# Attention stage of a two-layer decoder step: transposes and value products three units behind the scores, exponentials one unit behind

## The chip, the cores and the metric

The kernel runs as one program on one core of a Trainium2 chip. The metric is the device time of one execution in microseconds. A core has TensorE for matrix products (PE in the profile; PEld are its weight loads), VectorE (DVE), ScalarE (ACT), GpSimd (POOL), and SyncE (SP), which here only issues DMAs.

## The reference, cut to what matters

The program is one inference step of a decoder with two layers, for a prompt of 1024 rows and eight samples of one row. Layer 0 is RWKV-7 mixing and an MLP, then shared keys and values are projected, and layer 1 is differential attention over them and an MLP. The change touches the attention stage alone. For the prompt, that stage computes for each of 8 heads and each block of 128 query rows

```python
s = jnp.einsum('bqhmd,bkhmd->bhmqk', qi, k).astype(jnp.float32) * ATTN_SCALE   # m: two maps per head
s = jnp.where(k_pos[None, :] <= q_pos[:, None], s, NEG)
p = jax.nn.softmax(s, axis=-1)
attn = p[..., 0, :, :] - lam * p[..., 1, :, :]
o = jnp.einsum('bhqk,bkhe->bqhe', attn, v)
```

and each row of `o` is divided by its root mean square and scaled. For the samples it does the same with one query row each over 1024 past keys and values, which lie in pages of 128 rows that a table names, 64 pages in all.

## The kernel before, in words

`attention_phase` runs five instruction streams, one for each engine, that meet only in semaphores; each engine executes its own stream in order. The work is cut into 64 units (`NU`): unit u is head u // 8 and one block of 128 query rows, in the order of `ORDER`, so that a unit has 8, 1, 7, 2, 6, 3, 5, 4 blocks of keys in turn. Even units are "long" (5 to 8 blocks), odd ones "short" (1 to 4). The two kinds have buffers of their own: the scores of a long unit lie in four PSUM banks, those of a short one in two, and there is one buffer for the probabilities, one for the combined probabilities (`at`, in the profile att_attn_long and att_attn_short) and one for their transposed blocks (`aT`, att_attn_cols) of each kind. All transposes, of whatever, go through one PSUM bank, `tb`, and ScalarE must copy it out before TensorE may fill it again; all value products go through one bank, `ob`. In the profile both are named aux.

Every stream loops over u from 0 to `END` - 1. With w = u - 2 an iteration does:

- TensorE: transposes of the first four blocks of unit w (L2088, through `turn4`), the score products of unit u for both maps and the causal mask (L2106, L2110), transposes of the other blocks of w, then `extras(u)`, then the value products of w (L2120). The extras are transposes of the next head's keys and values (`rows`), of the finished head's output (`fin`), and for the samples page score transposes and, from unit 38 on, every third unit, value products of a sample (`page_v`, L2155) and a fold of their result (`page_cols`, L2162).
- VectorE: the maximum of the scores of unit u (L2231) and its negative scaled (L2233), a page sum (L2250), `combine(u - 1)`, which is a reciprocal (L2239), a ratio of one element per row (L2241) and the combined probabilities (L2245), and a second page sum.
- ScalarE: copies of the transposed blocks of w (L2355), copies for the extras, the scaled output of w (`take`, L2362), the exponentials of unit u for both maps (L2347).
- GpSimd: for u below 32, two products of a page of past keys with a query row (L2072), each into one of two buffers that VectorE's page sums read; and once a head the squares of its output (L2078).
- SyncE: loads of the next head, of key pages four ahead, and of value pages.

What orders the two sides is a few waits in this code: TensorE's transposes of w wait for `combine(w)`, its score products of u for the exponentials of u - 2, ScalarE's exponentials for L2233 of the same unit.

```python
            for u in range(END):
                w = u - 2
                live = 0 <= w < NU
                if live:
                    need(pe, "attn", w + 1)
                    turn4(("attn", w, 0), [...])
                if u < NU:
                    scores(u)
```

## Time and profile before

| | us |
|---|---|
| median of 3 runs (lowest, highest) | 4176.69 (4170.09, 4177.06) |
| the profiled execution: its time | 4166.23 |
| its span, first to last instruction | 4164.5 |
| attention stage in it, first DMA issue to the next stage's first | 2593.1 to 3205.8 |
| TensorE busy over the span (share) | 3483.6 (84%) |
| VectorE, ScalarE, GpSimd busy | 1899.8, 1346.4, 1563.1 |

Times in the trace count from the start of the span. The attention stage is 612.7 us of it. A row of a timeline gives the start, the time taken, the engine, the line of the code, the operation with output and input, and in brackets how long the engine had been idle and what released it. Consecutive instructions of VectorE overlap by a little under 0.1 us in such rows, so that what an instruction costs its engine is the distance to the start of the next. A row of a view of waits gives the waiting instruction and the one it waited for, then the total, the number of waits and the longest. The score product of unit u is recognised by the maximum that follows it (L2231).

### The profile page before, as it was taken

How to read it: one execution, taken by the hardware profiler on the slowest of the kernel's cores; microseconds unless marked ns; L12 is line 12 of the kernel's file. 1: busy time of each engine (PE TensorE's matmuls, PEld its weight loads, DVE VectorE, ACT ScalarE, POOL GpSimd, SP SyncE). 2: the span in 40 equal slices, each digit the busy share in tenths (PEclk: the TensorE clock that was granted, in tenths of full speed). 3: DMA queues.
4: the chain of work that ended last, by engine and by line, in shares of the span. 5: the costliest groups of instructions: out<-in, count | busy, mean ns of one | idle time of the engine just before them, and what ended most of it. 6: DMA issues, size and time to landing. Idle time of an engine off the chain costs nothing. (4 is left out here: it accounts for less than half of the span.)

```text
span 4164.5 us, 78261 instructions
## 1 busy us (share of the span) xinstructions
PE 3483.6 (84%) x34038; PEld 3147.2 (76%) x34038; DVE 1899.8 (46%) x2159; ACT 1346.4 (32%) x2059; POOL 1563.1 (38%) x648
## 2 busy tenths in 40 slices
PE   5889686898897298999999999455775989999896
PEld 2888435888786188999999998333443889999896
DVE  3333606455542586353454430677433772522622
ACT  1111113433432134333333433333444333333332
POOL 0111000000000155656656665455000656556563
PEclk8999858999998599999999999667887999999998
DMA  5222123334331543445444665545353534444442
GB/s 191 83 85 73 46 92 126 122 113 149 114 105 48 167 124 115 133 131 152 141 138 140 183 188 158 193 152 202 137 202 102 163 104 139 127 138 140 125 141 71
DMA packets 710476, 546.83 MB, mean 131 GB/s; under 512 B 34763, under 2 KB 667491, under 8 KB 709885
## 3 DMA queue, kind: packets, MB, share of 16 engines
q1 hardware_dynamic: 664182, 473.18, 36.9%
q10 hardware_dynamic: 45606, 67.55, 4.7%
q8 instruction: 266, 4.36, 0.4%
q0 software_dynamic: 352, 1.18, 0.1%
q14 instruction: 70, 0.57, 0.0%
HBM read 471.55 MB, written 70.29 MB: 130 GB/s over the span
## 5 line engine op out<-in xcount | busy, mean ns | idle before, releaser
L1630 POOL TENSOR_TENSOR dense_w_lo<-dense_w_raw,dense_w_hi 128x1024 fp32r<-128x1024 f32 x504 | 1273.4, 2532 | 974.8 <-ACT dense_w_hi L1701 974.6
L1686 PE MATMUL acc<-dense_x_hi,dense_w_hi 128*128 128x344 f32 x2496 | 813.2, 330 | 86.2 <-DVE dense_x_lo L1791 41.4
L1687 PE MATMUL acc<-dense_x_lo,dense_w_hi 128*128 128x344 f32 x2496 | 802.3, 326 | 0.0
L1701 ACT ACTIVATE dense_w_hi<-dense_w_raw 128x1024 fp32r<-128x1024 f32 x504 | 531.1, 1056 | 628.8 <-PE acc L1691 536.0
L1686 PEld LDWEIGHTS acc<-dense_x_hi,dense_w_hi 128*128 128x128 f32 x2496 | 482.4, 193 | 98.6 <-issue 79.7
L1687 PEld LDWEIGHTS acc<-dense_x_lo,dense_w_hi 128*128 128x128 f32 x2496 | 482.6, 193 | 2.5 <-issue 0.9
L1686 PE MATMUL acc<-dense_hid_hi,dense_w_hi 128*128 128x344 f32 x1536 | 483.4, 319 | 0.5 <-DVE dense_hid_lo L1811 0.5
L1687 PE MATMUL acc<-dense_hid_lo,dense_w_hi 128*128 128x344 f32 x1536 | 483.4, 319 | 0.0
L1691 PE MATMUL acc<-dense_x_hi,dense_w_lo 128*128 128x344 f32 x2496 | 449.7, 323 | 1.3 <-POOL dense_w_lo L1630 1.3
L1691 PEld LDWEIGHTS acc<-dense_x_hi,dense_w_lo 128*128 128x128 f32 x2496 | 409.9, 190 | 2.1 <-POOL dense_w_lo L1630 1.8
L750 POOL TENSOR_TENSOR x0T<-nT,levels 128x512 f32<-128x512 f32 x16 | 29.7, 1855 | 744.0 <-DVE bR L1249 744.0
L1686 PEld LDWEIGHTS acc<-dense_hid_hi,dense_w_hi 128*128 128x128 f32 x1536 | 288.4, 188 | 1.1 <-DVE dense_hid_lo L1811 1.1
L1687 PEld LDWEIGHTS acc<-dense_hid_lo,dense_w_hi 128*128 128x128 f32 x1536 | 288.2, 188 | 0.0
L170 PE MATMUL acc<-mix_hi,w_hi 128*128 128x344 f32 (+2 forms) x672 | 221.7, 330 | 76.8 <-DVE mix_lo L538 61.4
L1807 DVE TENSOR_TENSOR dense_relu<-dense_relu 128x344 f32<-128x344 f32 x192 | 148.6, 774 | 292.8 <-ACT dense_relu L1717 292.5
L1826 DVE SCALAR_TENSOR_TENSOR z<-acc,mods,z 128x344 f32<-128x344 f32 (+1 forms) x144 | 81.1, 568 | 431.5 <-PE acc L1691 431.5
L1691 PE MATMUL acc<-dense_hid_hi,dense_w_lo 128*128 128x344 f32 x1536 | 274.2, 321 | 1.0 <-POOL dense_w_lo L1630 1.0
L1691 PEld LDWEIGHTS acc<-dense_hid_hi,dense_w_lo 128*128 128x128 f32 x1536 | 249.5, 188 | 1.6 <-POOL dense_w_lo L1630 1.6
L1717 ACT ACTIVATE dense_relu<-acc 128x344 f32<-128x344 f32 x192 | 87.4, 455 | 460.4 <-PE acc L1691 362.4
L2072 POOL TENSOR_TENSOR att_k_prod<-att_k_page,att_q_row_all 128x1024 f32<-128x1024 f32 x64 | 153.4, 2400 | 176.0 <-DVE att_scores L2250 144.8
L171 PE MATMUL acc<-mix_lo,w_hi 128*128 128x344 f32 (+2 forms) x672 | 217.9, 324 | 0.0
L172 PE MATMUL acc<-mix_hi,w_lo 128*128 128x344 f32 (+2 forms) x672 | 217.7, 324 | 0.0
(384 smaller groups left out, 5983.6 us busy)
## 6 DMA issues: line engine op xcount, KB each, us to landing
dense_w_raw<-in_ffn_w SPq DMA_DIRECT2D x384, 512.0 KB, 4.1
ada_quarter<-in_ada_w SPq DMA_DIRECT2D x40, 1024.0 KB, 11.0
att_k_page<-in_cache_k SPq DMA_DIRECT2D x64, 512.0 KB, 3.6
att_v_page<-in_cache_v SPq DMA_DIRECT2D x64, 512.0 KB, 5.9
scratch_mix<-proj_stage ACTq DMA_DIRECT2D x48, 516.0 KB, 2.7
scratch_mix<-dense_stage ACTq DMA_DIRECT2D x72, 172.0 KB, 2.1
w_raw<-in_a_w_rkv SPq DMA_DIRECT2D x24, 512.0 KB, 4.2
dense_w_raw<-in_a_w_o SPq DMA_DIRECT2D x24, 512.0 KB, 4.5
```

What stands on the lines that cost most here:

```text
L170: m.nc.tensor.matmul(out, hi, xh[:, k, cols], start=(k == 0), stop=False)
L171: m.nc.tensor.matmul(out, hi, xl[:, k, cols], start=False, stop=False)
L172: last = m.nc.tensor.matmul(out, lo, xh[:, k, cols], start=False, stop=(k == KC - 1))
L1630: nc.gpsimd.tensor_tensor(wlo[:, i % NW], raw[:, i % NRAW], whi[:, i % NW].bitcast(F32), ALU.subtract).then_inc(S("lo"), 1)
L1686: T_.matmul(out, whi[:, s % NW, k, :], a, start=j.first and k == 0, stop=False)
L1687: T_.matmul(out, whi[:, s % NW, k, :], b, start=False, stop=False)
L1691: last = T_.matmul(out, wlo[:, s % NW, k, :], a, start=False, stop=j.last and k == KC - 1)
L1701: A(whi[:, i % NW], raw[:, i % NRAW], ACT.Copy).then_inc(S("hi"), 1)
L1717: A(t[:, n % 2, :], bank(jobs[s].acc), ACT.Relu).then_inc(S("taken"), 1)
L1807: V.tensor_tensor(tt, tt, tt, ALU.mult).then_inc(S("hid_sq"), 1)
L1826: V.scalar_tensor_tensor(zk, ps[:, 0:w], m.mod(gt, j.mo), zk, ALU.mult, ALU.add).then_inc(S("added"), 1)
L2072: nc.gpsimd.tensor_tensor(prod[:, j % 2, :], kp[:, j % NK, :], qb[:, b % 2, :], ALU.mult).then_inc(S("prod"), 1)
```

## The change

The lag of transposes and value products behind the scores becomes `LAG` = 3 in every stream, and what has to live longer gets more buffers: two combined-probability buffers of each kind, four slots for maxima, sums and ratios. With an odd lag, the transposes of a short unit meet the scores of a long one. ScalarE issues the exponentials of unit u - 1 in iteration u, map 0 behind the first copy of transposed blocks and map 1 behind the second. TensorE splits the value products of a long unit in two, and puts the first extra of an iteration between the parts, or, with a short unit, ahead of its value products. GpSimd's page products get a third buffer (`NR`). The ratio becomes a `tensor_scalar` with two column operands. At the start of the stage the mask, keys and queries are loaded first, and the scores of unit 0 go ahead of the sample transposes, which now share four banks. The once-a-head steps of the output's root mean square move one unit later.

```diff
-        NK, NV = 4, 12
+        NK, NV, NR = 4, 12, 3
...
-        END = NU + 10
+        END, LAG = NU + 10, 3
...
-        at = (sb("attn_long", [P, SEQ]), sb("attn_short", [P, SEQ // 2]))
+        at = (sb("attn_long", [P, 2, SEQ]), sb("attn_short", [P, 2, SEQ // 2]))
...
-        mx, nb, l, rl, w1 = (sb(x, [P, 2, 2]) for x in ("max", "neg_max", "sums", "weights", "ratio"))
+        mx, nb, l, rl, w1 = (sb(x, [P, 4, 2]) for x in ("max", "neg_max", "sums", "weights", "ratio"))
...
-        kp, prod = sb("k_page", [P, NK, D]), sb("k_prod", [P, 2, D])
+        kp, prod = sb("k_page", [P, NK, D]), sb("k_prod", [P, NR, D])
...
+        def attn_of(u):
+            return at[kind(u)][:, (u // 2) % 2]
+
+        def pages_of(u):
+
+            return range(min(NPAGE, 2 * u), min(NPAGE, 2 * u + 2))
...
-            nc.sync.dma_start(tab[:], io["page_table"].rearrange("(o b) n -> o (b n)", o=1)).then_inc(S("table_in"), 16)
+            nc.sync.dma_start(causal[:], io["masks"][:, C_CAUSAL:C_CAUSAL + P]).then_inc(S("mask_in"), 16)
+            nc.sync.dma_start(k[:, 0], m.scr[S_K, 0, :, 0:SEQ]).then_inc(S("in_k"), 16)
+            nc.sync.dma_start(q[:, 0], m.scr[S_R, 0, :, 0:SEQ]).then_inc(S("in_q"), 16)
             for t, row in ((qs, S_R), (ks, S_K), (vs, S_V)):
                 nc.sync.dma_start(t[:], m.scr[row, :, :, SEQ:T].rearrange("c p n -> p c n")).then_inc(S("cols_in"), 16)
-            nc.sync.dma_start(k[:, 0], m.scr[S_K, 0, :, 0:SEQ]).then_inc(S("in_k"), 16)
-            nc.sync.dma_start(q[:, 0], m.scr[S_R, 0, :, 0:SEQ]).then_inc(S("in_q"), 16)
+            nc.sync.dma_start(tab[:], io["page_table"].rearrange("(o b) n -> o (b n)", o=1)).then_inc(S("table_in"), 16)
             nc.sync.dma_start(v[:], m.scr[S_V, 0, :, 0:SEQ]).then_inc(S("in_v"), 16)
-            nc.sync.dma_start(causal[:], io["masks"][:, C_CAUSAL:C_CAUSAL + P]).then_inc(S("mask_in"), 16)
             for i, name in enumerate(("b_lam_q", "b_lam_k")):
...
-                if u < KU:
-                    for j in (2 * u, 2 * u + 1):
-                        b = j // NP
-                        pool.wait_ge(S(f"k_in{j % NK}"), 16 * (j // NK + 1))
-                        if j % NP == 0:
-                            pool.wait_ge(S(f"qb{b % 2}"), 16 * (b // 2 + 1))
-                        need(pool, "red", j - 1)
-                        nc.gpsimd.tensor_tensor(prod[:, j % 2, :], kp[:, j % NK, :], qb[:, b % 2, :], ALU.mult).then_inc(S("prod"), 1)
-                if u % KC == 2 and u > 2:
+                for j in pages_of(u):
+                    b = j // NP
+                    pool.wait_ge(S(f"k_in{j % NK}"), 16 * (j // NK + 1))
+                    if j % NP == 0:
+                        pool.wait_ge(S(f"qb{b % 2}"), 16 * (b // 2 + 1))
+                    need(pool, "red", j - NR + 1)
+                    nc.gpsimd.tensor_tensor(prod[:, j % NR, :], kp[:, j % NK, :], qb[:, b % 2, :], ALU.mult).then_inc(S("prod"), 1)
+                if u % KC == 3 and u > 3:
                     h = u // KC - 1
                     if h < NH:
...
-            def values(w):
+            def values(w, part):
                 h, n = w // KC, blocks(w)
-                need(pe, "take", w)
-                need(pe, "t_in", nth["rows", h, 3] + 1)
-                for j in range(n):
-                    if j % 4 == 0:
-                        need(pe, "t_in", nth["attn", w, j // 4] + 1)
+                if part == 0:
+                    need(pe, "take", w)
+                    need(pe, "t_in", nth["rows", h, 3] + 1)
+                need(pe, "t_in", nth["attn", w, part] + 1)
+                for j in range(4 * part, min(n, 4 * part + 4)):
                     last = T_.matmul(ob[:, 0:P], aT[kind(w)][:, j * P:(j + 1) * P], vrow[:, h % 2, j, :],
                                      start=(j == 0), stop=(j == n - 1))
-                last.then_inc(S("o_mm"), 1)
+                if j == n - 1:
+                    last.then_inc(S("o_mm"), 1)
...
+            need(pe, "consts", 2)
+            need(pe, "in_k", 16)
+            scores(0)
             pe.wait_ge(S("cols_in"), 48)
-            for i, t in enumerate((qs, ks, vs)):
-                for h in range(NH):
-                    last = T_.transpose((m.acc[0], m.acc[1], m.aux2)[i][0:NS, h // 4, (h % 4) * P:(h % 4 + 1) * P], t[:, h, :], m.ident[:])
-            last.then_inc(S("qkv_t"), 1)
-            need(pe, "sample_rows", 3)
+            sample_turn(qs, six[:, 4:6, :])
+            sample_turn(ks, m.aux2)
+            need(pe, "sample_rows", 1)
+            sample_turn(vs, six[:, 4:6, :])
+            need(pe, "sample_rows", 2)
             need(pe, "consts", 4)
             for part in range(4):
                 head_rows(0, part)
+            need(pe, "sample_rows", 3)
             for u in range(END):
-                w = u - 2
+                w = u - LAG
                 live = 0 <= w < NU
                 if live:
                     need(pe, "attn", w + 1)
-                    turn4(("attn", w, 0), [at[kind(w)][:, j * P:j * P + P] for j in range(min(4, blocks(w)))])
-                if u < NU:
+                    turn4(("attn", w, 0), [attn_of(w)[:, j * P:j * P + P] for j in range(min(4, blocks(w)))])
+                if 0 < u < NU:
                     scores(u)
+                todo = extras(u)
                 if live and blocks(w) > 4:
-                    turn4(("attn", w, 1), [at[kind(w)][:, j * P:j * P + P] for j in range(4, blocks(w))])
-                for name in extras(u):
+                    turn4(("attn", w, 1), [attn_of(w)[:, j * P:j * P + P] for j in range(4, blocks(w))])
+                    values(w, 0)
+                elif live and todo:
+                    extra(todo.pop(0))
+                    values(w, 0)
+                elif live:
+                    values(w, 0)
+                if live and blocks(w) > 4:
+                    if todo:
+                        extra(todo.pop(0))
+                    values(w, 1)
+                for name in todo:
                     extra(name)
-                if live:
-                    values(w)
```

On VectorE (buffer indices aside) and on ScalarE:

```diff
             def combine(u):
-                kd, n = kind(u), blocks(u) * P
+                kd, c, n = kind(u), u % 4, blocks(u) * P
                 need(dve, "exp", 2 * u + 2)
-                need(dve, "take", u - 1)
-                V.reciprocal(rl[:, kd, :], l[:, kd, :]).then_inc(S("rl"), 1)
+                need(dve, "take", u - 3)
+                V.reciprocal(rl[:, c, :], l[:, c, :]).then_inc(S("rl"), 1)
                 need(dve, "rl", u + 1)
-                V.scalar_tensor_tensor(w1[:, kd, 0:1], rl[:, kd, 1:2], lam[:, 0:1], l[:, kd, 0:1], ALU.mult, ALU.mult).then_inc(S("ratio"), 1)
+                V.tensor_scalar(w1[:, c, 0:1], rl[:, c, 1:2], l[:, c, 0:1], lam[:, 0:1], ALU.mult, ALU.mult).then_inc(S("ratio"), 1)
                 need(dve, "ratio", u + 1)
-                if u >= 2:
-                    need(dve, "t_mm", nth[attn_rounds(u - 2)[-1]] + 1)
-                V.scalar_tensor_tensor(at[kd][:, 0:n], pm[kd][:, 1, 0:n], w1[:, kd, 0:1], pm[kd][:, 0, 0:n], ALU.mult,
+                if u >= 4:
+                    need(dve, "t_mm", nth[attn_rounds(u - 4)[-1]] + 1)
+                V.scalar_tensor_tensor(attn_of(u)[:, 0:n], pm[kd][:, 1, 0:n], w1[:, c, 0:1], pm[kd][:, 0, 0:n], ALU.mult,
                                        ALU.add).then_inc(S("attn"), 1)
...
-                if u < KU:
-                    page_sums(2 * u + 1)
-                if r == 3 and 1 <= h <= NH:
+                for j in todo:
+                    page_sums(j)
+                if r == 4 and 1 <= h <= NH:
                     need(dve, "osq", h)
                     need(dve, "rrms", h - 1)
                     V.tensor_reduce(ss[:], osq[:], AX.X, ALU.add).then_inc(S("ss"), 1)
-                if r == 4 and 1 <= h <= NH:
+                if r == 5 and 1 <= h <= NH:
                     need(dve, "rms", h)
                     need(dve, "on", h - 1)
                     V.reciprocal(rs[:], ss[:]).then_inc(S("rrms"), 1)
...
-            need(act, "qkv_t", 1)
-            for i in range(3):
-                A(rows[:, i, :].rearrange("p (a n) -> p a n", a=2), (m.acc[0], m.acc[1], m.aux2)[i][0:NS, 0:2, :],
-                  ACT.Copy).then_inc(S("sample_rows"), 1)
+            for i, banks in enumerate((six[:, 4:6, :], m.aux2, six[:, 4:6, :])):
+                need(act, "qkv_t", i + 1)
+                A(rows[:, i, :].rearrange("p (a n) -> p a n", a=2), banks[0:NS], ACT.Copy).then_inc(S("sample_rows"), 1)
...
-            def exps(u):
-                kd, n = kind(u), blocks(u) * P
+            def exps(u, maps):
+                kd, c, n = kind(u), u % 4, blocks(u) * P
                 need(act, "nb", u + 1)
                 need(act, "attn", u - 1)
-                for mp in range(2):
-                    A(pm[kd][:, mp, 0:n], scores_of(u, mp), ACT.Exp, bias=nb[:, kd, mp:mp + 1], scale=ATTN_SCALE,
-                      accum_out=l[:, kd, mp:mp + 1]).then_inc(S("exp"), 1)
+                for mp in maps:
+                    A(pm[kd][:, mp, 0:n], scores_of(u, mp), ACT.Exp, bias=nb[:, c, mp:mp + 1], scale=ATTN_SCALE,
+                      accum_out=l[:, c, mp:mp + 1]).then_inc(S("exp"), 1)
...
             for u in range(END):
-                w = u - 2
-                for name in attn_rounds(w):
-                    turned(name)
+                w = u - LAG
+                for i in range(2):
+                    for name in attn_rounds(w)[i:i + 1]:
+                        turned(name)
+                    if 1 <= u <= NU:
+                        exps(u - 1, (i,))
                 for name in extras(u):
                     extra(name)
                 if 0 <= w < NU:
                     take(w)
-                if u < NU:
-                    exps(u)
                 h, r = divmod(u, KC)
-                if r == 3 and 1 <= h <= NH:
+                if r == 4 and 1 <= h <= NH:
                     need(act, "ss", h)
                     A(ss[:], ss[:], ACT.Sqrt, bias=eps[:, 0:1], scale=1.0 / P).then_inc(S("rms"), 1)
```

On TensorE before, two iterations near the end of the second head, a long unit's transposes beside a long unit's scores and a short one's beside a short one's. The rows are iteration 14 (w = 12, scores of 5 blocks) and 15 (w = 13, scores of 4); att_o is the `fin` extra:

```order
L2088 MATMUL aux<-ident,att_attn_long 128x128 x4
L2106 MATMUL acc<-att_k,att_q 128x512 x2
L2106 MATMUL acc<-att_k,att_q 128x128 x2
L2110 MATMUL acc<-att_causal_r,att_eye_r 128x128 x2
L2088 MATMUL aux<-ident,att_attn_long 128x128 x2
L2088 MATMUL aux<-ident,att_o 128x128 x4
L2120 MATMUL aux<-att_v_rows,att_attn_cols_long 128x128 x6
L2088 MATMUL aux<-ident,att_attn_short 128x128 x3
L2106 MATMUL acc<-att_k,att_q 128x512 x2
L2110 MATMUL acc<-att_causal_r,att_eye_r 128x128 x2
L2088 MATMUL aux<-ident,att_o 128x128 x4
L2120 MATMUL aux<-att_v_rows,att_attn_cols_short 128x128 x3
```

There the extra stands ahead of all value products, and a turn of the bank follows a turn of the bank. In the changed kernel iterations 13 (w = 10, scores of 3 blocks) and 14 (w = 11, scores of 5 blocks); att_v is a `rows` extra:

```order
L2093 MATMUL aux<-ident,att_attn_long 128x128 x4
L2111 MATMUL acc<-att_k,att_q 128x384 x2
L2115 MATMUL acc<-att_causal_r,att_eye_r 128x128 x2
L2093 MATMUL aux<-ident,att_attn_long 128x128 x3
L2125 MATMUL aux<-att_v_rows,att_attn_cols_long 128x128 x4
L2093 MATMUL aux<-ident,att_v 128x128 x4
L2125 MATMUL aux<-att_v_rows,att_attn_cols_long 128x128 x3
L2093 MATMUL aux<-ident,att_attn_short 128x128 x2
L2111 MATMUL acc<-att_k,att_q 128x512 x2
L2111 MATMUL acc<-att_k,att_q 128x128 x2
L2115 MATMUL acc<-att_causal_r,att_eye_r 128x128 x2
L2093 MATMUL aux<-ident,att_o 128x128 x4
```

The value products (L2125) now stand between two uses of the transpose bank, and the seven blocks of the long unit w = 10 are transposed beside the short scores. On ScalarE before, iterations 14 and 15; att_probs are the exponentials, att_out_cols the copies of the `fin` extra:

```order
L2355 ACTIVATE att_attn_cols_long<-aux 128x512
L2355 ACTIVATE att_attn_cols_long<-aux 128x256
L2373 ACTIVATE att_out_cols<-aux,att_subln_g 128x512
L2362 ACTIVATE att_o<-aux,att_weights 128x128
L2347 ACTIVATE att_probs_long,att_sums<-acc,att_neg_max 128x640 x2
L2355 ACTIVATE att_attn_cols_short<-aux 128x384
L2373 ACTIVATE att_out_cols<-aux,att_subln_g 128x512
L2376 DMA scratch_mix<-att_out_cols 128x1024
L2362 ACTIVATE att_o<-aux,att_weights 128x128
L2347 ACTIVATE att_probs_short,att_sums<-acc,att_neg_max 128x512 x2
```

Both maps stand behind `take` (L2362). In the changed kernel the same engine, iterations 15 and 16, from the first copy of transposed blocks of w = 12:

```order
L2379 ACTIVATE att_attn_cols_long<-aux 128x512
L2371 ACTIVATE att_probs_long,att_sums<-acc,att_neg_max 128x640
L2379 ACTIVATE att_attn_cols_long<-aux 128x256
L2371 ACTIVATE att_probs_long,att_sums<-acc,att_neg_max 128x640
L2397 ACTIVATE att_out_cols<-aux,att_subln_g 128x512
L2400 DMA scratch_mix<-att_out_cols 128x1024
L2386 ACTIVATE att_o<-aux,att_weights 128x128
L2379 ACTIVATE att_attn_cols_short<-aux 128x384
L2371 ACTIVATE att_probs_short,att_sums<-acc,att_neg_max 128x512 x2
L2386 ACTIVATE att_o<-aux,att_weights 128x128
```

The exponentials of the long unit 14 are now one map behind each copy, and `take` comes last.

## Rows read from the trace of the kernel before

**Rows 1.** Busy us by stretch: PE, PEld, DVE, ACT, POOL, TensorE clock, DMA share, GB/s

```profile
2618.40:2925.80 307.40, 168.99 (x754) 109.89 (x754) 234.12 (x231) 102.77 (x235) 154.42 (x66) 0.69 0.51 177
2925.80:3181.90 256.10, 200.60 (x1151) 127.19 (x1150) 96.23 (x178) 116.87 (x267) 7.57 (x4) 0.83 0.39 138
```

**Rows 2.** Waits, VectorE and TensorE, 2771.8 to 2850.3: total us, times, longest

```profile
DVE att_max L2231 <- PE acc L2110: 21.1, 8, 4.2
PE aux L2088 <- DVE att_attn_long L2245: 20.0, 4, 6.0
PE aux L2088 <- DVE att_attn_short L2245: 12.5, 4, 5.7
```

**Rows 3.** Timeline, VectorE and GpSimd, one unit: start, us taken, engine, line

```profile
2778.56 1.21 DVE L2250 TENSOR_REDUCE att_scores<-att_k_prod 128x16 f32<-128x1024 f32 x1
...
2779.91 2.35 POOL L2072 TENSOR_TENSOR att_k_prod<-att_k_page,att_q_row_all 128x1024 f32<-128x1024 f32 x1 [2.08 <-DVE att_scores L2250]
...
2781.20 0.42 DVE L2231 TENSOR_REDUCE att_max<-acc 128x2 f32<-128x256 f32 x1 [1.43 <-PE acc L2110]
...
2781.65 0.63 DVE L2233 TENSOR_SCALAR att_neg_max<-att_max 128x2 f32<-128x2 f32 x1
...
2782.20 1.20 DVE L2250 TENSOR_REDUCE att_scores<-att_k_prod 128x16 f32<-128x1024 f32 x1
...
2783.52 2.39 DVE L2241 SCALAR_TENSOR_TENSOR att_ratio<-att_weights,att_neg_lambda,att_sums 128x1 f32<-128x1 f32 x1
...
2783.55 2.34 POOL L2072 TENSOR_TENSOR att_k_prod<-att_k_page,att_q_row_all 128x1024 f32<-128x1024 f32 x1 [1.29 <-DVE att_scores L2250]
...
2785.94 1.28 DVE L2245 SCALAR_TENSOR_TENSOR att_attn_long<-att_probs_long,att_ratio 128x1024 f32<-128x1024 f32 x1
...
2787.14 1.21 DVE L2250 TENSOR_REDUCE att_scores<-att_k_prod 128x16 f32<-128x1024 f32 x1
```

**Rows 4.** Lines of VectorE, 2925.8 to 3181.9: count, busy us, mean ns, idle before

```profile
L2231 DVE TENSOR_REDUCE att_max<-acc 128x2 f32<-128x2048 f32 (+7 forms) x32 | 43.4, 1357 | 152.8 <-PE acc L2110 152.8
...
L2245 DVE SCALAR_TENSOR_TENSOR att_attn_long<-att_probs_long,att_ratio 128x1024 f32<-128x1024 f32 (+3 forms) x15 | 16.5, 1098 | 0.5
...
L2245 DVE SCALAR_TENSOR_TENSOR att_attn_short<-att_probs_short,att_ratio 128x512 f32<-128x512 f32 (+3 forms) x16 | 8.8, 552 | 0.6
...
L2233 DVE TENSOR_SCALAR att_neg_max<-att_max 128x2 f32<-128x2 f32 x31 | 5.2, 169 | 1.1
...
L2272 DVE TENSOR_TENSOR att_o<-att_o,att_rms 128x1024 f32<-128x1024 f32 x4 | 4.9, 1225 | 0.1
```

**Rows 5.** Timeline of the stage's start (columns as in Rows 3)

```profile
2604.78 1.90 ACT L2320 ACTIVATE att_v_page<-acc 8x1024 f32<-8x1024 f32 x2
...
2613.87 4.65 POOL L2072 TENSOR_TENSOR att_k_prod<-att_k_page,att_q_row_all 128x1024 f32<-128x1024 f32 x2 [31.15 <-DMA att_q_row_all<-scratch_sample_y]
...
2635.11 2.02 DVE L2231 TENSOR_REDUCE att_max<-acc 128x2 f32<-128x1792 f32 x1 [3.76 <-PE acc L2110]
```

**Rows 6.** Waits of TensorE, 2925.8 to 3181.9 (columns as in Rows 2)

```profile
PE aux L2088 <- ACT att_attn_cols_short L2355: 13.7, 8, 2.6
PE aux L2088 <- ACT att_attn_cols_long L2355: 7.8, 12, 0.8
PE aux L2120 <- ACT att_attn_cols_short L2355: 6.3, 3, 2.5
PE aux L2155 <- ACT att_page_o L2388: 5.7, 8, 0.7
PE aux L2088 <- DVE att_attn_short L2245: 3.2, 2, 2.5
```

**Rows 7.** Lines of ScalarE, 2925.8 to 3181.9 (columns as in Rows 4)

```profile
L2347 ACT ACTIVATE att_probs_long<-acc,att_neg_max 128x1024 f32<-128x1024 f32 (+3 forms) x32 | 30.2, 950 | 1.0 <-DVE att_neg_max L2233 0.9
```

**Rows 8.** Timeline, one group of score products at either clock

```profile
2749.33 2.51 PE L2106 MATMUL acc<-att_k,att_q 64*128 64x512 f32 x8
...
2965.75 1.35 PE L2106 MATMUL acc<-att_k,att_q 64*128 64x512 f32 x8
```

30 lines of the change are left out of this document (17 added, 13 removed).

## The prediction, put on record before the changed kernel ran

> **What bounds the kernel now.** The busy times by stretch come first. The attention stage has two parts. In the first, from the maximum of unit 0 to that of unit 32 (307.4 us, 9.6 a unit), no engine is full: TensorE 169.0 us at a granted clock of 0.69, VectorE 234.1, GpSimd 154.4. In the second, to the maximum of unit 63 (256.1 us, 8.3 a unit), TensorE is busy for 200.6 us and nobody else for half the time [rows 1]. So the question is who waits for whom, and in the third head, a period of 78.5 us for eight units, the views of waits answer it: VectorE waits 21.1 us for score products (8 waits, of which one of 4.2 belongs to the period before, so 17), TensorE 32.5 us for combined probabilities [rows 2]. They take turns. TensorE's score products of unit u stand behind the transposes of u - 2, these behind `combine(u - 2)`, this behind the maximum of u - 1. A ring over both engines is what bounds the first part.
>
> VectorE has a second partner. In the timeline, each page sum (L2250) that ends lets GpSimd start its next page product 0.14 us later, and the product takes 2.34. While it runs, the reciprocal and the reductions keep their times, but the negative maximum took 0.63 us instead of 0.17, and the ratio, one element per row, took 2.39 and ended with the product [rows 3, 4] (the 0.17 is the mean of the second part, where GpSimd is idle). So two small things of a unit can each be held until a product ends.
>
> **First part, step by step.** With a lag of 3, TensorE's transposes in iteration u need `combine(u - 3)`, a whole iteration of VectorE earlier, and its score products need only the exponentials of u - 2. It gets ahead, and VectorE's wait for the scores goes: this alone would be 17 us a head. What is late next is VectorE itself with GpSimd. One unit, from the start of its preceding page sum, in distances between starts [rows 3]: the page product that this sum releases ran from 1.35 to 3.70 (2778.56 to 2779.91 and 2782.26); the maximum starts at 1.13 (the sum's 1.21 less the overlap) and takes 1.36 on average [rows 4], for a long unit of 8 blocks 2.3 by my estimate (eight forms from 0.42 for one block, in proportion); the negative maximum is held by the product, so the next page sum starts at 3.64 (2778.56 to 2782.20) whatever the size of the unit. Before, an idle wait stood in the place of much of this hold, 1.43 us in this unit. From there to the combined probabilities 3.74 (2782.20 to 2785.94, again the length of a product), then their own 0.74, the mean of 1.10 and 0.55 [rows 4] less the overlap of 0.08. Sum 8.12 us a unit. The ratio as a `tensor_scalar` changes nothing here: if it isn't held, the combined probabilities behind it are, by the same product; between 0 and 0.03 us a unit.
>
> Once a head come a multiplication of 1.23 us [rows 4] that waits for a product first, 2.8 us together beyond what a unit has anyway, and, estimated from the same holds, 1.5 us for GpSimd's squares in the middle of its products and for ScalarE's square root, which now waits in the middle of the stream for a sum that stands at the end of VectorE's iteration, with the exponentials of the next unit behind it. So a head takes 8 x 8.12 + 4.3 = 69.3 us. The third buffer of page products gains nothing: no row shows VectorE waiting for a product. From the maximum of unit 2 (2635.1 [rows 5]) to that of unit 32 (2925.8) there are 30 units and three such sets: 243.6 + 12.9 = 256.5 for 290.7, that is -34.
>
> Can TensorE keep up? Its busy time is 169.0 over 32 units, 5.3 a unit, all at the low clock; with a bare wait for the bank (0.7, below) twice a unit it needs 6.7 of 8.1. Yes, with 1.4 to spare.
>
> The start: the score products of unit 0 go ahead of the sample transposes, which ScalarE's copies (2604.8) wait for; eight score products take 2.51 us at the low clock [rows 8], and so I put the query row, and GpSimd's first product (2613.9 [rows 5]), 2.6 us later, at 2616.5. Two page products (4.65 [rows 5]) and a sum behind it the maximum of unit 1 is at 2622.3, and that of unit 2, after one normal unit, at 2630.4 for 2635.1, where it had waited 3.76 us for its scores: -5, with bounds of 0 and -8. First part: -39. Its bounds are 0 (the hold eats all that the idle gave) and -73 (17 us a head, and 5).
>
> **Second part.** Here VectorE waits for scores (152.8 us [rows 4]) and has no say. TensorE is idle for 256.1 - 200.6 = 55.5 us [rows 1]. Three kinds [rows 6]. Eleven waits, 13.7 + 6.3 = 20.0 us, 1.8 each, are for copies of a short unit's blocks: ScalarE has just begun the exponentials of a long unit, 0.95 us a map [rows 7], and they stand ahead of the copy. In the new order at most one map stands there, and score products or value products are between; I take them down to a bare round trip of 0.7: -12. The waits for combined probabilities, 3.2 us and smaller ones, go: -4. The rest, some 31 us, are bare round trips through the one bank, 0.65 (7.8 over 12) to 0.71 (5.7 over 8) each. Value products now stand between two of them in most iterations, but only one to four of them. Half goes: -15. Against that, ScalarE's wait for the sum of squares in the middle of its stream, 1.5 us four times: +6. Second part: -25, bounds +12 (each of 16 long units waits 0.75 more for a copy behind an exponential) and -55 (no idle time left). The tail after unit 63 has the same work with one iteration without scores more: 0, up to +2.
>
> **The sum.** -39 - 25 = -64 us on the profiled execution: 4166.2 to 4102. The median of the runs is 4176.7, 10.5 above the profiled one; the forecast in terms of the median is 4113.
>
> **Rivals.**
> 1. VectorE's idle time goes in full, because the products of GpSimd fall elsewhere than at the negative maximum. For it: with a third buffer GpSimd has a product more in hand and need not start one at the end of every sum. Against: it has 8.1 us for 4.7 us of work, so it is always caught up, and starts at a sum's end as in both cases of rows 3. -73 - 25 = -98: 4079. Chance 0.10.
> 2. The second part gives nothing: ScalarE's stream is in order, and a copy that had the exponentials of another unit ahead of it now has a map of its own iteration ahead. -39: 4138. Chance 0.16.
> 3. The clock rises as above: 4098. Chance 0.17.
> 4. Slower: the exponentials of u - 1 stand between the two copies of ScalarE, so TensorE's value products and its next bank wait for the negative maximum of u - 1, and the score products of u + 1 come behind them. If that ring (negative maximum, two maps 1.9, copy 0.6, extra, value products and transposes 4, scores 2.5, maximum 1.4, hold 2.3, and waits of 0.1 to 0.2 between closes once for every unit instead of once in two, it is about 13.7 us against 9.6 now in the first part. It decides from the point where more than one unit in five closes it (4.1 us lost against 1.0 gained). With half the units of the first part, 16 x 4.1 - 16 x 1.5 - 5 = +37, and no gain in the second: 4214. Against it: score products of u + 1 need the exponentials of u - 1 only, and by the order of the streams these are issued an iteration earlier. Chance 0.04.
> 5. The lag has no effect since page products and VectorE's own work fill the time that TensorE's part leaves: within 0.2% of now, 4177. Chance 0.03.
>
> **From these the numbers.** The forecast has 0.50, with a range of its own of 4095 to 4130. The range of 4078 to 4150 takes in the clock, the full recovery of the idle time and a second part without gain. All cases but the last two are faster by more than 0.2% (8 us, about what a measurement here can tell from no change): 0.93; 0.03 the same; 0.04 slower.
>
> **What would show it.** In the first part: no wait of VectorE for score products beyond a few, no wait of TensorE for combined probabilities longer than 1 us, the negative maximum at about 1 us on average for 0.45, a distance of 8.1 us between maxima. A distance of 7 would be rival 1, over 9 rival 4 or 5. In the second: TensorE's idle time at 30 us for 55, its waits for copies of short units near 0.7 each; the clock still near 0.83. The forecast is wrong if VectorE still waits for scores in the first part, or if ScalarE shows waits for the negative maximum in most units.

## The result, and the profile after

| | median us | lowest to highest | runs |
|---|---|---|---|
| before | 4173.4 | 4166.5 to 4177.1 | 4 |
| after | 4075.7 | 4070.8 to 4078.5 | 4 |

The ratio is 0.9767, 95% interval 0.9749 to 0.9784: 97.7 us faster, where 64 were forecast, and 2.3 us below the low end of the range. In the two profiled executions the attention stage, from its first DMA issue to the next stage's first, shrank from 612.7 to 515.4 us, by 97.3. The times of these two executions differ by 89.6 us, since in the changed kernel's the stage began 8.7 us later. Such shifts of the stage's start, up to 12.5 us, came between the traces of this study, whatever the kernel. So stretches of the stage are compared, not spans.

| stretch, from maximum to maximum | before | after | change | forecast |
|---|---|---|---|---|
| stage's start to unit 2 | 42.0 | 35.1 | -6.9 | -5 |
| first part, unit 2 to 32 | 290.7 | 235.5 | -55.2 | -34 |
| second part, unit 32 to 63 | 256.1 | 221.9 | -34.2 | -25 |
| tail | 23.9 | 22.9 | -1.0 | 0 |

First the changed kernel's busy times by stretch (columns as in [rows 1], whose first row begins 16.7 us earlier, at unit 0). First part, then second:

```profile
2636.94:2872.43 235.49, 144.04 (x720) 101.78 (x719) 226.39 (x221) 96.31 (x224) 149.20 (x63) 0.76 0.65 218
2872.43:3094.30 221.87, 181.61 (x1146) 117.18 (x1147) 99.33 (x179) 115.86 (x266) 7.58 (x4) 0.89 0.45 159
```

In the first part VectorE is now busy for 226.4 of 235.5 us, counting the time in which an instruction of it is held by GpSimd's product: it is the bound. In the second TensorE idles for 40.3 us (221.9 - 181.6), and its clock is 0.89.

The waits of the third head, 2746.3 to 2810.85, a period of 64.6 us where it was 78.5:

```profile
POOL att_k_prod L2077 <- DVE att_scores L2274: 24.1, 15, 2.4
...
PE aux L2093 <- DVE att_attn_long L2269: 11.9, 3, 4.9
ACT att_ss L2436 <- DVE att_ss L2291: 11.3, 1, 11.3
PE aux L2093 <- ACT att_attn_cols_long L2379: 9.8, 3, 7.3
```

VectorE's wait for score products, first in [rows 2] with 21.1, is gone: the view has no row of it. TensorE waits instead, for VectorE's combined rows and for the copies behind ScalarE's square root, and that costs nothing while VectorE is the bound. Where VectorE's time went over the whole first part is told by its lines. Before:

```profile
L2241 DVE SCALAR_TENSOR_TENSOR att_ratio<-att_weights,att_neg_lambda,att_sums 128x1 f32<-128x1 f32 x30 | 52.2, 1741 | 1.1
L2231 DVE TENSOR_REDUCE att_max<-acc 128x2 f32<-128x1792 f32 (+7 forms) x31 | 43.0, 1387 | 69.8 <-PE acc L2110 69.8
L2245 DVE SCALAR_TENSOR_TENSOR att_attn_long<-att_probs_long,att_ratio 128x896 f32<-128x896 f32 (+3 forms) x15 | 29.9, 1990 | 0.5
L2233 DVE TENSOR_SCALAR att_neg_max<-att_max 128x2 f32<-128x2 f32 x30 | 12.9, 430 | 1.0
L2245 DVE SCALAR_TENSOR_TENSOR att_attn_short<-att_probs_short,att_ratio 128x128 f32<-128x128 f32 (+3 forms) x15 | 8.1, 538 | 0.5
```

And after:

```profile
L2255 DVE TENSOR_REDUCE att_max<-acc 128x2 f32<-128x1792 f32 (+7 forms) x31 | 42.6, 1373 | 0.1
L2269 DVE SCALAR_TENSOR_TENSOR att_attn_long<-att_probs_long,att_ratio 128x896 f32<-128x896 f32 (+3 forms) x15 | 35.3, 2352 | 0.5
L2269 DVE SCALAR_TENSOR_TENSOR att_attn_short<-att_probs_short,att_ratio 128x128 f32<-128x128 f32 (+3 forms) x15 | 34.8, 2323 | 0.5
L2257 DVE TENSOR_SCALAR att_neg_max<-att_max 128x2 f32<-128x2 f32 x30 | 32.7, 1089 | 1.0
L2265 DVE TENSOR_SCALAR att_ratio<-att_weights,att_sums,att_neg_lambda 128x1 f32<-128x1 f32 x30 | 8.2, 273 | 1.1
L2263 DVE RECIPROCAL att_weights<-att_sums 128x2 f32<-128x2 f32 x30 | 4.5, 150 | 5.7 <-ACT att_probs_long L2371 5.7
```

Read by rows: the wait before the maximum -69.7; the negative maximum +19.8, since GpSimd's product now falls upon it more often; ratio and combined probabilities together from 90.2 to 78.3, -11.9; a new wait of the reciprocal for exponentials +5.7. Their sum, -56.1, is nearly the whole of -55.2. The new wait comes once a head, 1.9 us, where the exponentials stand behind the square root (the 11.3 of ScalarE in the waits above). The holds can be seen in one unit (columns as in [rows 3]):

```profile
2746.20 2.27 DVE L2255 TENSOR_REDUCE att_max<-acc 128x2 f32<-128x2048 f32 x1
...
2748.71 1.21 DVE L2274 TENSOR_REDUCE att_scores<-att_k_prod 128x16 f32<-128x1024 f32 x1
...
2750.03 0.27 DVE L2265 TENSOR_SCALAR att_ratio<-att_weights,att_sums,att_neg_lambda 128x1 f32<-128x1 f32 x1
2750.06 2.34 POOL L2077 TENSOR_TENSOR att_k_prod<-att_k_page,att_q_row_all 128x1024 f32<-128x1024 f32 x1 [1.29 <-DVE att_scores L2274]
...
2750.33 2.62 DVE L2269 SCALAR_TENSOR_TENSOR att_attn_short<-att_probs_short,att_ratio 128x512 f32<-128x512 f32 x1
...
2752.87 1.21 DVE L2274 TENSOR_REDUCE att_scores<-att_k_prod 128x16 f32<-128x1024 f32 x1
...
2754.00 0.41 DVE L2255 TENSOR_REDUCE att_max<-acc 128x2 f32<-128x256 f32 x1
...
2754.22 2.35 POOL L2077 TENSOR_TENSOR att_k_prod<-att_k_page,att_q_row_all 128x1024 f32<-128x1024 f32 x1 [1.82 <-DVE att_scores L2274]
2754.45 2.15 DVE L2257 TENSOR_SCALAR att_neg_max<-att_max 128x2 f32<-128x2 f32 x1
...
2756.51 1.21 DVE L2274 TENSOR_REDUCE att_scores<-att_k_prod 128x16 f32<-128x1024 f32 x1
```

From page sum to page sum over the maximum it is 3.64 (2752.87 to 2756.51), the forecast's number; over the combination 4.16 (2748.71 to 2752.87), where the forecast had 4.48. The ratio runs beside the product's start and isn't held (0.27). The 512-wide combination is, 2.62 for 0.75 alone, and ends 0.55 after the product.

TensorE's waits in the second part, against [rows 6]:

```profile
PE aux L2093 <- ACT att_attn_cols_long L2379: 8.0, 7, 1.9
PE aux L2093 <- ACT att_page_o L2412: 6.5, 8, 0.8
...
PE aux L2093 <- DMA att_k<-scratch_mix: 3.7, 1, 3.7
PE aux L2093 <- DVE att_scores L2274: 3.2, 1, 3.2
PE aux L2093 <- ACT att_attn_cols_short L2379: 2.8, 1, 2.8
```

The 20.0 us for copies of short units are one wait of 2.8 now. Two waits are new, 3.7 for the next head's keys and 3.2 for a page sum.

### The profile page after: what moved, and what is told of

Same layout as the page of the kernel before. It is cut to its first block and busy times, and to the rows that moved or that the text cites. A ratio compares the mean times of both kernels' runs of the same rounds, so it can differ in the third digit from the quotient of the medians.

```text
span 4074.8 us, 78319 instructions
## 1 busy us (share of the span) xinstructions
PE 3456.6 (85%) x34038; PEld 3143.4 (77%) x34038; DVE 1907.8 (47%) x2159; ACT 1343.3 (33%) x2059; POOL 1564.8 (38%) x648
```

## The experiments

All are edits of the changed kernel but one. Each ratio is to runs of the kernel before that were taken beside it (medians 4171.7 to 4172.7). Part lengths are from one trace each, from maximum 2 to 32 to 63; the changed kernel has 235.5 and 221.9. TensorE's and ScalarE's work of the second part is the same in seven further traces (the runs with the old ratio, the small products, the column, the split, the two with two buffers, and both sums behind the combination), where it took 212.5 to 221.0. The changed kernel's own 221.9 is the longest of the eight, so a difference under 10 us in the second part says nothing.

**The ratio as it was.**

```diff
-V.tensor_scalar(w1[:, c, 0:1], rl[:, c, 1:2], l[:, c, 0:1], lam[:, 0:1], ALU.mult, ALU.mult)
+V.scalar_tensor_tensor(w1[:, c, 0:1], rl[:, c, 1:2], lam[:, 0:1], l[:, c, 0:1], ALU.mult, ALU.mult)
```

> The changed kernel with the ratio again as scalar_tensor_tensor of two tensors; nothing else. Theory (hold): as a tensor_scalar of one element the ratio is never held by a page product, and the combined probabilities behind it overlap about 0.24 us of their own start with the end of the product. So with the old form the 32 units of the first part take 0.24 us more each: +7 to +8 us, ratio rows near 2.4 us instead of 0.27, page sum to page sum over the combination back at 3.74 plus the combination's own time. Rival (my prediction's figure): whichever of the two is held ends with the same product, 0 to +1 us.

Measured: 4085.5, ratio to before 0.9787 (0.9772 to 0.9803); first part 249.2, 13.7 longer, where 7 to 8 were expected. The ratio is held, and the combination behind it runs alone. In the unit with GpSimd's squares there is a second price:

```profile
2761.00 2.39 DVE L2265 SCALAR_TENSOR_TENSOR att_ratio<-att_weights,att_neg_lambda,att_sums 128x1 f32<-128x1 f32 x1
...
2763.43 0.75 DVE L2269 SCALAR_TENSOR_TENSOR att_attn_short<-att_probs_short,att_ratio 128x512 f32<-128x512 f32 x1
2764.09 1.21 DVE L2274 TENSOR_REDUCE att_scores<-att_k_prod 128x16 f32<-128x1024 f32 x1
...
2777.65 2.40 DVE L2265 SCALAR_TENSOR_TENSOR att_ratio<-att_weights,att_neg_lambda,att_sums 128x1 f32<-128x1 f32 x1
...
2780.00 1.89 POOL L2083 TENSOR_TENSOR att_o_sq<-att_o 128x1024 f32<-128x1024 f32 x1
2780.09 1.95 DVE L2269 SCALAR_TENSOR_TENSOR att_attn_short<-att_probs_short,att_ratio 128x128 f32<-128x128 f32 x1
```

4.40 from sum to sum for 4.16 in the ordinary unit (0.24 us a unit, 7.2 us over 30); in the other the ratio waits for the product and the combination for the squares. There it is 5.62 for 3.78, 1.84 three times, 5.5 us. Together 12.7 of the 13.7. The prediction put this term at 0 to 0.03 us a unit.

**A lag of 2, all else kept.**

```diff
-        END, LAG = NU + 10, 3
+        END, LAG = NU + 10, 2
```

> The changed kernel with LAG = 2; all other edits stay (two more combined-probability buffers, exponentials in the next iteration, split value products, third page buffer, new start). Theory (ring): VectorE's wait for scores in the first part returns, since transposes of u - 2 and with them the scores of u wait for the combination made in the iteration before: at least the first part's 55 us go back, and as the exponentials are issued an iteration later than in the kernel before, the ring is longer than before: 4150 to 4220. Rival (buffers and order): the gain came from the buffers and the order of issue, and the time stays within 20 us of 4076.

Measured: 4148.9 (0.9952, 0.9936 to 0.9969). First part 285.5, within 5.2 of before, second 241.0. In 75 us of one head (2770 to 2845) the ring is back:

```profile
DVE att_max L2255 <- PE acc L2115: 16.7, 7, 3.7
...
PE aux L2093 <- DVE att_attn_short L2269: 15.8, 4, 5.5
```

So the lag of 3 is what removes the ring, worth 50.0 us in the first part. The time lies just below the expected 4150 to 4220, and the kernel was not slower than before, as the upper part of that range would have it.

**The placements in the second part.** Exponentials together and in their own unit; value products in one piece behind the extra; and both, with the old ratio, so that only the lag is left:

```diff
-    for i in range(2):
-        for name in attn_rounds(w)[i:i + 1]:
-            turned(name)
-        if 1 <= u <= NU:
-            exps(u - 1, (i,))
+    for name in attn_rounds(w):
+        turned(name)
...
+    if u < NU:
+        exps(u, (0, 1))
```

> The changed kernel with the exponentials of unit u again at the end of ScalarE's iteration u, both maps together, behind take; all else stays. Theory: in the first part VectorE and the page products bound, and nothing moves (7.9 us a unit, +-5 us in all). In the second part copies of transposed blocks stand behind two exponentials again: TensorE idles 10 to 20 us more and its clock is lower; 4085 to 4105. Rival: the interleaving is worth nothing, 4076 within 4.

```diff
-    elif live and todo:
-        extra(todo.pop(0))
-        values(w, 0)
...
+    if live:
+        values(w, 0)
+        if blocks(w) > 4:
+            values(w, 1)
```

> The changed kernel with TensorE's old order inside an iteration: transposes, scores, transposes, all extras, then all value products. Theory: first part unchanged; in the second part the value products no longer cover round trips through the transpose bank, 15 us more idle time of TensorE: 4085 to 4095. Rival: the value products' place is worth nothing since ScalarE's exponentials set the copies, 4076 within 4.

> The changed kernel with three parts undone: exponentials of unit u at the end of iteration u, all extras ahead of all value products, and the ratio as scalar_tensor_tensor. What is left is the lag of 3 with its buffers, the third page buffer and the new start. Theory: the lag alone buys the first part, 249 us for 30 units as with the old ratio (291 before), and in the second part next to nothing, 250 to 256 us for 31 units (256 before): the two placements work there together. In all 4120 to 4130. Rival: the placements are two ways to the same gain, either one undone costs 22 us and both undone no more: second part 244 us, 4112.

| | median us | ratio (interval) | first part | second part | TensorE idle there | its clock |
|---|---|---|---|---|---|---|
| exponentials as before | 4104.3 | 0.9839 (0.9819 to 0.9858) | 235.0 | 244.9 | 52.5 | 0.85 |
| value products as before | 4100.1 | 0.9820 (0.9802 to 0.9839) | 236.5 | 244.3 | 47.4 | 0.81 |
| lag alone | 4137.0 | 0.9923 (0.9906 to 0.9941) | 249.4 | 267.2 | 60.6 | 0.79 |

The placements do nothing for the first part, where the lag alone gives 41.3 of the 55.2 us and the ratio the rest. In the second each gives 22 to 23 us; together 45. That is against the longest of the eight traces; against their mean, 217, they give some 5 us more. Only part of it is idle time of TensorE. Undoing the exponentials adds 12.3 us of idle and 10.8 of busy time, undoing the value products 7.2 and 15.3 (15 of idle time were expected), both at a lower clock. The lag alone makes the second part 11 us longer than before (267.2 for 256.1, and 257.9 in the other trace of the old order), which no expectation had. With the exponentials in their old place the copy of a long unit waits behind them:

```profile
PE aux L2093 <- ACT att_attn_cols_long L2379: 27.0, 12, 3.6
...
PE aux L2093 <- ACT att_attn_cols_short L2379: 4.2, 4, 1.4
```

These are all of TensorE's waits for copies of transposed blocks there, 31.2 us; in the changed kernel all such waits add up to 14.2 (11.4 for long units, 2.8 for the short). So 17 us of waits came back, while the idle time as a whole grew by 12.3. That step of the forecast (-12 for copies behind exponentials) had the right mechanism, and with the lag of 3 there is more of it to save, since the lag moves the trouble from the short unit to the long one: before, the waits for copies were 22.7 for short units and 9.1 for long; with the lag alone 6.6 and 33.1.

**Is the hold the bound?** GpSimd multiplies 64 of 1024 elements of each page, so this kernel leaves out most of the samples' scores:

> The changed kernel whose GpSimd products cover 64 of the 1024 columns (the rest of the three buffers is filled once with ones), so the sample outputs are not the reference's; VectorE's page sums stay whole. It measures the hold. Theory: without a product of 2.3 us under way the negative maximum takes 0.2 us and the combined probabilities their own time, VectorE's own work is some 5.3 us a unit, and TensorE with its waits at some 6 sets the pace: first part of 30 units 165 to 190 us instead of 235. Rival: VectorE's own work and the wait for exponentials fill the 7.8 us, the hold only takes the place of a wait: over 215 us.

Measured 3995.7 in one run; the first part:

```profile
L2259 DVE TENSOR_SCALAR att_neg_max<-att_max 128x2 f32<-128x2 f32 x30 | 5.2, 175 | 1.0
```

167.8 us for 235.5, with the negative maximum at 0.175 for 1.089. VectorE is busy for 157.9 us there for 226.4: the negative maxima are 27.5 us less, the combined probabilities 40.8 (29.3 for 70.1). VectorE waits for no product from maximum 2 to 32 in either trace. So 68 us of the first part are holds. It is a single run, and what less reading and writing by GpSimd does elsewhere isn't separated.

**Which of the instructions can be held.** The negative maximum with its factor from a column, and as two instructions of one element a row:

```diff
-V.tensor_scalar(nb[:, c, :], mx[:, c, :], -ATTN_SCALE, None, ALU.mult)
+V.tensor_scalar(nb[:, c, :], mx[:, c, :], eps[:, 2:3], None, ALU.mult)
```

> The changed kernel with the negative maximum's factor from a column of SBUF and not an immediate, two elements per row as before. The ratio, a tensor_scalar with two column operands and one element, was never held (0.27 us in every unit). Theory A: it's the column operand that frees an instruction from the hold: negative maximum rows at 0.2 us for 1.09, first part 15 to 25 us shorter. Theory B: it's the single element: nothing moves, 1.0 to 1.1 us, time within 5 us of 4076.

```diff
+V.tensor_scalar(nb[:, c, 0:1], mx[:, c, 0:1], -ATTN_SCALE, None, ALU.mult)
+V.tensor_scalar(nb[:, c, 1:2], mx[:, c, 1:2], -ATTN_SCALE, None, ALU.mult)
```

> The changed kernel with the negative maximum as two tensor_scalar instructions of one element per row each, with the immediate. Theory B (an instruction of one element isn't held): the two take 0.2 us each, the page sum behind them starts at about 2.9 instead of 3.64 us into a unit with a short maximum, and the product that it releases starts as soon as the one before it ends: 7.1 to 7.4 us a unit for 7.8, first part 12 to 22 us shorter than 235, in all 4055 to 4065. Theory A (only the column operand frees it): the first of the two is held as now, 0.1 us a unit more, 4076 to 4082.

The column: 4076.8 (0.9772, 0.9756 to 0.9788), first part 235.6. It is still held:

```profile
L2258 DVE TENSOR_SCALAR att_neg_max<-att_max,att_eps 128x2 f32<-128x2 f32 x30 | 33.0, 1099 | 1.1
```

The split: 4041.1 (0.968, 0.9664 to 0.9697), first part 202.6, 33 us shorter, where 12 to 22 were expected. In its first part:

```profile
L2270 DVE SCALAR_TENSOR_TENSOR att_attn_long<-att_probs_long,att_ratio 128x896 f32<-128x896 f32 (+3 forms) x15 | 25.9, 1730 | 0.5
...
L2257 DVE TENSOR_SCALAR att_neg_max<-att_max 128x1 f32<-128x1 f32 x30 | 4.6, 154 | 1.0
L2258 DVE TENSOR_SCALAR att_neg_max<-att_max 128x1 f32<-128x1 f32 x30 | 4.3, 144 | 0.0
```

Neither half is held in any of the units. 23.8 us come from there (32.7 to 8.9) and 9.4 from the long units' combination (35.3 to 25.9). In the changed kernel it started 0.27 us into a product in most units; now it mostly starts 1.3 us or more into one, or beside none. The short units' costs 2.0 more.

**The spare product buffer.** Two in place of three, in the changed kernel and in the split one:

```diff
-        NK, NV, NR = 4, 12, 3
+        NK, NV, NR = 4, 12, 2
```

> The changed kernel with two page product buffers again instead of three. Theory: VectorE waited for no product before and GpSimd has 7.9 us a unit for 4.7 us of products, so a third buffer gains nothing in the steady state: head periods 64.6 us within 0.5. A few us may come at the start, where three products run ahead: units 2 to 8 at up to 49 us for 44.6. In all 4076 to 4081. Rival: the third buffer is what keeps VectorE from waiting once it no longer waits for scores: head periods 2 us or more longer, 4085 or more.

> The negative maximum as two one-element instructions (the run of 4041) with two product buffers. There a unit takes 6.9 us for 4.7 of products, and GpSimd is nearer to the pace. Theory: with two buffers a product can start only when the sum before last is done, so a product often starts just ahead of the combined probabilities and holds them its whole length: head period 55 goes to 57 or more, 4050 to 4060. Rival: no effect, 4041 within 4.

4068.6 (0.9749, 0.9718 to 0.9779), first part 236.2: the third buffer gives nothing, as forecast. Inside the part two things cancel: units 2 to 8 took 47.8 us for 44.6, and the first two heads 63.3 each for 64.6. The stage is as long as with three buffers (515.5 for 515.4), so the lower median, within the interval of the other, comes from outside it. With the split 4031.2 (0.9661, 0.9633 to 0.9689), first part 199.7. This is the lowest median of the study, though its interval overlaps the split kernel's; the expectation that it would be slower was wrong.

**The same two edits in the kernel before.**

> The kernel before, lag 2 and its orders, with only the two small VectorE instructions made free of the hold: the ratio as tensor_scalar of one element and the negative maximum as two of one element. Theory: in its ring the combination is on the path of every unit, so the 0.2 to 0.4 us of the ratio count, and the negative maximum's 0.27 too: 9.8 us a unit less 0.5, first part 291 to 275, in all 4150 to 4160. Rival: the hold is what bounds the first part in both kernels, and freeing these two gives as much as in the changed kernel or more: 4135 or less.

4163.1 (0.9975, 0.9959 to 0.9991), first part 282.2, 8.5 us shorter, where 16 were expected. VectorE still waits for TensorE, 71.2 us for 69.8, and the hold goes from the ratio (52.2 to 8.2) to the combination behind it (29.9 and 8.1 before):

```profile
L2231 DVE TENSOR_REDUCE att_max<-acc 128x2 f32<-128x1792 f32 (+7 forms) x31 | 43.0, 1388 | 71.2 <-PE acc L2110 71.2
L2246 DVE SCALAR_TENSOR_TENSOR att_attn_long<-att_probs_long,att_ratio 128x896 f32<-128x896 f32 (+3 forms) x15 | 42.4, 2824 | 0.5
L2246 DVE SCALAR_TENSOR_TENSOR att_attn_short<-att_probs_short,att_ratio 128x128 f32<-128x128 f32 (+3 forms) x15 | 36.3, 2423 | 0.5
L2242 DVE TENSOR_SCALAR att_ratio<-att_weights,att_sums,att_neg_lambda 128x1 f32<-128x1 f32 x30 | 8.2, 273 | 1.1
```

By the medians the two edits are worth 8.6 us there and 44 in the changed kernel (9.8 for the ratio and 34.6 for the split). The split has little to free inside the ring: there the negative maximum mostly came when the product was over, and took 12.9 us in all (8.9 split), while with the ring gone it took 32.7.

**Both page sums behind the combination**, in the split kernel:

> The run of 4041 with both page sums of a unit behind the combination instead of one ahead and one behind. Theory: the products that the two sums release run back to back for 4.7 us from 1.35 us after the first sum's start; the combined probabilities reach the port at about 4.3 us and are held to 6.05, so a unit is 6.7 us for 6.9 now: 4034 to 4040. Rival: VectorE gets the port between the two products, the hold ends at 3.7 and costs nothing, unit at TensorE's pace of about 6 us: 4010 to 4025. Second rival: the sums come so late that GpSimd falls behind and VectorE waits for products: over 4045.

4036.4 (0.9679, 0.965 to 0.9708), first part 195.9, stage 467.4 us, the shortest (with two buffers and the split 474.3). The median doesn't tell it from the two kernels before it.

## Why the prediction had the ring right and the gain too small

**The ring, and what comes late next.** Right: with the lag VectorE's 69.8 us of waits go, and the negative maximum rises to 1.09 us, forecast at about 1; the distance between maxima is 7.85 us on average, forecast at 8.1. A lag of 2 brings the ring back. One sign that the prediction named failed: it had no wait of TensorE for combined probabilities over 1 us, and in the third head alone there are three, up to 4.9. Its own sum says why: TensorE had 1.4 us a unit to spare, and waits for the engine that bounds.

**The ratio.** This is the step that failed: "The ratio as a `tensor_scalar` changes nothing here: if it isn't held, the combined probabilities behind it are, by the same product; between 0 and 0.03 us a unit." The hold did move to the combination, but a held combination costs less than a held ratio and a combination behind it, and in the unit with squares there were two holds. Measured 13.7 us for a first part of 30 units by undoing it (0.46 a unit), of the 21 by which the first part beat its forecast. The 1.5 forecast for the squares is in this: with the old ratio they do cost about that (5.62, where 3.74 and 0.27 for the 128-wide combination make 4.0), with the new one nothing.

**The rest of the first part**, 7 us, is two terms. With the old ratio, units 2 to 8 take 49.3 us for 48.7 forecast, the first two heads 67.7 each for 69.3, and the third 64.4. The 1.6 of each head are the multiplication. It was put at 2.8, a wait for a product and its own time; it got in with the product instead:

```profile
2794.34 1.22 DVE L2297 TENSOR_TENSOR att_o<-att_o,att_rms 128x1024 f32<-128x1024 f32 x1
2794.34 3.44 POOL L2077 TENSOR_TENSOR att_k_prod<-att_k_page,att_q_row_all 128x1024 f32<-128x1024 f32 x1 [2.21 <-DVE att_scores L2274]
```

It took 1.22, in all three heads (mean of L2297 in the first part 1224 ns), and the product 1.1 more than its 2.35. The trace of before had shown the same in two heads of three (1.22 and 1.23; 2.02 in the third, which makes its mean of 1491). The third head's other 3.3 are its last unit: the 64 page products are over by then, nothing is held, and from sum to sum it takes 2.45 over the maximum and 2.38 over the combination, 4.8 for the 8.1 that the forecast gave to all 30 units.

**The start.** -6.9 for -5, with the first product 3.0 us later against the stage's start, forecast at 2.6.

**The second part.** TensorE's idle time fell by 15.2 (55.5 to 40.3), where 25 was forecast. The term that failed is the one for bare round trips through the bank, "Half goes: -15". In the views of waits of both traces, those for copies of short units went from 22.7 to 2.8 and those for combined probabilities from 4.8 to none, more than the 12 and 4 forecast. All other waits for copies were 28.0 before (43 waits) and are 32.3 (48 waits), and 7.9 for keys and for VectorE are new. The placement of the value products does cover some waits (without it those for copies of long units are 21.4 for 11.4), but only such as the lag had added.

TensorE's busy time fell by 19.0 (200.6 to 181.6) with practically the same instructions, at a clock of 0.89 for 0.83. That is the third rival, priced at 15, and it came on top of the forecast instead of in its place. The 9 us by which this part beat its forecast are such a gain that wasn't in the sum, less what didn't come of the idle time. They lie within the 10 us between traces of the same work; by the mean of these, 217, it is 14. Whether less idling causes the higher clock is not shown: over the traces the two mostly go together (idle 36.6 at 0.90, 40.3 at 0.89, 50.3 at 0.84, 55.5 at 0.83, 60.6 at 0.79), but 52.5 stands at 0.85 and 47.4 at 0.81, and no run changed one without the other.

**The rivals.** The first had nearly the number, 4079, by luck and for a reason that isn't so: VectorE's idle time did not come back in full, the hold ate 19.8 us of it, and gains from elsewhere made up for that. The second (no gain in the second part) is refuted: -34.2, and undoing either placement takes most of that away. The fourth's ring didn't close: VectorE waited 5.7 us in all for exponentials, and no wait for scores was left. The fifth is refuted by -97.7 us. Two factors of the working are off by little: the clock's 0.44 is 0.46 by its own rows (1.35 for 2.51), and the fourth rival takes 1.0 us as the gain of a unit in one place and 1.5 in another.

**The error in sum.** 33 us: 14 the ratio, 7 the other terms of the first part (5 the multiplication, 3 the last unit, less 1), 2 the start, 1 the tail, and in the second part 9, which is 19 of busy time at the higher clock less 10 of idle time that stayed.

## What to carry to other kernels

When a ring over two engines goes, look at once at the small instructions of the engine that is now the bound: freeing two that a neighbour's long instruction could hold gave 8.6 us inside the ring and 44 outside it. Where two instructions in a row can be held, price the pair: freeing the first doesn't only hand its hold to the second. And undo each edit under the others as well as alone: here the lag alone cost 11 us in the stretch where its companions gained 45.

## What the runs showed of the hardware

- Whether a small VectorE instruction over SBUF is held by a GpSimd product went by its form. A `tensor_scalar` of 128x2 was (mean 1.09 us, up to 2.3, for 0.17), with its factor in the instruction or from a column alike; one of 128x1 never was (0.14 to 0.16 us in all 64 with a constant, 0.27 in all 64 with two columns, 30 of each beside a product), nor the reciprocal of 128x2 (0.15 to 0.17, with 23 begun inside a product in the split kernel). A `scalar_tensor_tensor` of 128x1 was (2.39 us for 0.22). The Trainium skill (VectorE: DVE Perf Modes, "Mode 2×_2P — use both read ports for one tensor") asks, for the mode that takes both ports, for an outermost non-unit dimension that is even, or odd and equal in source and destination. Read so that one element a row, which has no non-unit dimension, doesn't meet this, it agrees with the rows of the `tensor_scalar`; that the hold comes of this mode is not shown here.
- Where VectorE's multiplication and GpSimd's product began together (2794.34, and so in all three heads of the first part), VectorE's took its own 1.22 us and GpSimd's 3.44 for 2.35.
- Splitting one instruction of 0.17 us into two of 0.15 and 0.14, which overlap to 0.21, made the kernel 35 us faster.
